# A decode step's cache loads: thirteen key tiles ahead of the projection, nine per group, and value tiles of all kinds interleaved

## What is computed

```python
def mix_sample(x, win_k, win_v, sb_k_pool, sb_v_pool, mem_k, mem_v, page_table, mw):
    ...
    qa, ka, va, qb, kb, vb, qm = project_heads(rms_norm(x, g_pre), w_in)
    ...
    o_a = combine_by_denominators([dilated_group_gather(qa, k_all, v_all, n_buf, w, d) for w, d in DIL_PATTERNS])
    k_past = sb_k_pool[page_table].reshape(B, n_past, N_HEADS_SB, HEAD_DIM)
    v_past = sb_v_pool[page_table].reshape(B, n_past, N_HEADS_SB, HEAD_DIM)
    ...
    o_b = sweep_query_blocks(lambda q, qp: stick_breaking_block(q, kb_all, vb_all, qp, sb_bias), qb, pos)
    o_m = memory_attention(qm, mem_k, mem_v)
    y = mixer_output(x, o_a, o_b, o_m, g_out_a, g_out_b, g_out_m, w_out, g_post)
```

## Time and profile before

| | us |
|---|---|
| median of three runs | 2264.4 (2260.56 to 2265.96) |
| profiled execution, its own time | 2271.0 |
| its span, first to last instruction | 2269.2 |
| TensorE busy | 2153.5 (95%) |
| VectorE busy | 1340.9 (59%) |
| ScalarE busy | 919.0 (40%) |
| DMA, mean | 202 GB/s |

### The profile page before, as it was taken

One profiled execution on the slowest core, in us unless ns is written; L12 is line 12 of the kernel. 1 busy time (PEld: TensorE's weight loads), 2 busy tenths in 40 slices (PEclk: granted clock), 3 DMA queues, 4 the chain that ended last, 5 costly groups with the idle time before them and its releaser, 6 DMA issues.

```text
span 2269.2 us, 41305 instructions
## 1 busy us (share of the span) xinstructions
PE 2153.5 (95%) x16769; PEld 2042.6 (90%) x16769; DVE 1340.9 (59%) x3210; ACT 919.0 (40%) x1171; POOL 429.5 (19%) x369
## 2 busy tenths in 40 slices
PE   7999999999999999999967879899999999999996
PEld 6999999999999999999842339799999999999996
DVE  6555545555555686777783426575545565555656
ACT  3544434444343455343312414454434344343443
POOL 5200000000000043677501100440000000000004
PEclk9999999999999999999989979899999999999999
DMA  7454555555555546999999975345555555555551
GB/s 262 168 186 171 182 176 178 186 173 180 186 177 177 185 167 244 332 339 349 317 273 314 278 205 176 130 171 183 186 174 180 186 178 176 185 182 174 184 184 41
DMA packets 221536, 459.24 MB, mean 202 GB/s; under 512 B 11466, under 2 KB 12363, under 8 KB 220571
## 3 DMA queue, kind: packets, MB, share of 16 engines
q1 hardware_dynamic: 219874, 452.32, 59.2%
q0 software_dynamic: 1472, 4.29, 0.5%
HBM read 447.95 MB, written 8.62 MB: 201 GB/s over the span
## 4 chain that ended last, share of the span: by engine, by line
PE 49%; DMA 4%; DVE 3%; SPq 2%; issue 1%; POOL 1%; ACT 0%; POOLq 0%; DVEq 0%; ACTq 0%
PE ps L503 15%; PE ps L505 15%; PE ps L504 15%; DMA v_cache<-win_v 1%; SPq L427 1%; PE ps L809 1%; DMA v_cache<-sb_v 1%; SPq L426 1%; PE ps L684 1%; POOL acc L1736 1%; DVE y L1288 1%; DVE k_cache L1453 1%; DMA v_cache<-mem_v 1%; DMA k_cache<-win_k 0%; PE ps L782 0%
## 5 line engine op out<-in xcount | busy, mean ns | idle before, releaser
L1242 DVE TENSOR_TENSOR wl<-raw,wh 128x1024 fp32r<-128x1024 f32 x592 | 732.9, 1243 | 703.7 <-ACT wh L889 702.8
L889 ACT ACTIVATE wh<-raw 128x1024 fp32r<-128x1024 f32 x656 | 691.6, 1059 | 1029.6 <-PE ps L505 1005.1
L503 PE MATMUL ps<-xh,wh 128*128 128x264 f32 (+1 forms) x3776 | 1081.3, 286 | 17.7 <-DVE xl L1254 9.4
L505 PE MATMUL ps<-xh,wl 128*128 128x264 f32 (+1 forms) x3776 | 1077.9, 285 | 0.0
L504 PE MATMUL ps<-xl,wh 128*128 128x264 f32 (+1 forms) x3776 | 1077.8, 285 | 0.0
L503 PEld LDWEIGHTS ps<-xh,wh 128*128 128x128 f32 x3776 | 715.2, 189 | 20.8 <-issue 9.0
L505 PEld LDWEIGHTS ps<-xh,wl 128*128 128x128 f32 x3776 | 715.4, 189 | 0.0
L504 PEld LDWEIGHTS ps<-xl,wh 128*128 128x128 f32 x3776 | 714.9, 189 | 0.2
L503 PE MATMUL ps<-hh,wh 128*128 128x264 f32 x1408 | 400.8, 285 | 0.0
L505 PE MATMUL ps<-hh,wl 128*128 128x264 f32 x1408 | 399.9, 284 | 0.0
L504 PE MATMUL ps<-hl,wh 128*128 128x264 f32 x1408 | 399.1, 283 | 0.0
(11 more groups left out here) (227 smaller groups left out, 1159.8 us busy)
## 6 DMA issues: line engine op xcount, KB each, us to landing
raw<-w_gu SPq DMA_DIRECT2D x176, 1024.0 KB, 4.9
raw<-w_down SPq DMA_DIRECT2D x88, 1024.0 KB, 5.0
raw<-w_in SPq DMA_DIRECT2D x40, 1024.0 KB, 7.5
v_cache<-sb_v SPq DMA_DIRECT2D x128, 256.0 KB
k_cache<-sb_k SPq DMA_DIRECT2D x84, 256.0 KB
raw<-w_out SPq DMA_DIRECT2D x16, 1024.0 KB, 5.4
head_space<-sb_k SPq DMA_DIRECT2D x44, 256.0 KB
raw<-w_mem_kv SPq DMA_DIRECT2D x8, 1024.0 KB, 5.4
```

Of the source, the lines that this page charges most:

```text
L503: pe.matmul(out, w_hi, rh(k0 + kk), start=first and kk == 0, stop=False)
L505: mm = pe.matmul(out, w_lo, rh(k0 + kk), start=False, stop=last and kk == 1)
L889: act.activation(wh[:, c % UNIT_SLOTS], raw_unit(c), ACT.Copy).then_inc(hi_made, 1)
L1242: dve.tensor_tensor(wl[:, c % UNIT_SLOTS], raw_unit(c), wh[:, c % UNIT_SLOTS].bitcast(F32), ALU.subtract).then_inc(lo_made, 1)
```

## The change

- `FIRST_KEYS` = 13 key tiles are loaded before the steady part. Seven of them (2 to 8, `key_place` "early") have buffers of their own that are used once: three where `mem_space` was, four in the space of the feed-forward part's intermediates. Four tiles (0 to 3) are issued behind chunks 4 to 7 of the memory weights, tiles 4 to 8 behind projection chunks 0 to 4, tiles 9 to 12 after the parking.
- In the steady part three tiles instead of two follow every fourth chunk: nine for a group. VectorE takes projections after the tiles in `TAKE_AT`.
- Spreads 2 to 17 stand inside groups, ahead of the unit that `SPREAD_AT` names (group, unit); 18 to 31 stay behind the last group.
- `value_tile` mixes the kinds: two page tiles of sequence b + 1, then one window or memory tile of sequence b, and so on. There are ten value slots, the last three (`late_values`) over `k_cache` (the first load into them waits for all keys), and three banks for sums instead of two.

```diff
-ADD_AT = (11, 13, 19, 21, 35, 37, 43, 45)
+ADD_AT = (15, 17, 24, 26, 43, 45, 52, 54)
+TAKE_AT = (11, 20, 29, 39, 48, 57, 66, 74)
+SPREAD_AT = {2: (3, 0), 3: (3, 7), 4: (4, 6), 5: (5, 5), 6: (6, 4), 7: (7, 3), 8: (8, 2), 9: (8, 4), 10: (8, 5),
+             11: (8, 6), 12: (8, 7), 13: (9, 0), 14: (9, 1), 15: (9, 3), 16: (9, 5), 17: (9, 6)}
...
-V_SLOTS = 7
+FIRST_KEYS = 13
+V_SLOTS = 10
...
+def key_user(t):
+
+    if t >= FIRST_KEYS + K_SLOTS:
+        return t - K_SLOTS
+    return t - FIRST_KEYS if t < FIRST_KEYS + 2 else t - FIRST_KEYS + 7
...
 def value_tile(t):
 
-    if t < SB_TILES:
-        return divmod(t, PAGES // 2)
-    b, k = divmod(t - SB_TILES, 4)
-    return b, PAGES // 2 + k
+    if t < PAGES // 2:
+        return 0, t
+    b, r = divmod(t - PAGES // 2, 12)
+    if b == DEC - 1:
+        return b, PAGES // 2 + r
+    return (b + 1, r // 3 * 2 + r % 3) if r % 3 < 2 else (b, PAGES // 2 + r // 3)
...
-            for n in range(8):
-                load_pair(CH_MEM + n, n, w_mem_kv[0], slice(0, 2))
...
+            for n in range(8):
+                load_pair(CH_MEM + n, n, w_mem_kv[0], slice(0, 2))
+                if n == 4:
+                    sp.wait_ge(const_loaded, 16 * 9)
+                    sp.wait_ge(xl_ready["mem"], KT)
+                if n >= 4:
+                    load_keys(n - 4)
+            sp.wait_ge(unit_used, unit_of(CH_MEM))
             for n in range(10):
                 load_in(n)
-            sp.wait_ge(const_loaded, 16 * 9)
-            sp.wait_ge(xl_ready["mem"], KT)
-            for t in range(2):
-                load_keys(t)
+                if n < 5:
+                    load_keys(n + 4)
...
-            for t in range(2, K_SLOTS):
+            for t in range(9, FIRST_KEYS):
                 load_keys(t)
-            t = K_SLOTS
+            t = FIRST_KEYS
             for n in range(12, 44):
                 load_in(n)
-                load_keys(t)
-                load_keys(t + 1)
-                t += 2
+                for _ in range(3 if n % 4 == 3 else 2):
+                    load_keys(t)
+                    t += 1
...
             for t in range(TILES):
+                if t == V_SLOTS - 3:
+                    sp.wait_ge(k_used, TILES)
                 if t >= V_SLOTS:
                     sp.wait_ge(v_weighed, t - V_SLOTS + 1)
...
-                pe.wait_ge(in_read, 8 if f < 8 else 20 if f < 16 else 40)
+                pe.wait_ge(in_read, 8 if f < 8 else 20 if f < 18 else 40)
...
-                if k in (0, PAGES // 2) and number >= 2:
-                    pe.wait_ge(sum_taken, number - 1)
+                if k in (0, PAGES // 2) and number >= 3:
+                    pe.wait_ge(sum_taken, number - 2)
...
-            for t in range(SB_TILES):
+            for t in range(TAKE_AT[7] + 1):
                 take_scores(t)
-                if t % 8 == 7:
-                    take_projection(2 + t // 8)
+                if t in TAKE_AT:
+                    take_projection(2 + TAKE_AT.index(t))
```

More of the change, by code:

```diff
@@ L192, in decoder_step @@
             mask_far = sb("mask_far", [P, 2, SEQ], F32, part)
+        with ExitStack() as part:
+            early_a = sb("early_a", [P, 2, 1024], F32, part)
+            sb("first_keys_kept", [P, 1120], F32, part)
+            early_b = sb("early_b", [P, 2, 1024], F32, part)
         kv = sb("kv", [P, 24, TOK])
@@ L196, in decoder_step @@
             mem_space = sb("mem_space", [P, KT, N_MEM], F32, part)
+        with ExitStack() as part:
+            early_v = sb("early_v", [P, 3, 1024], F32, part)
         with ExitStack() as part:
@@ L250, in decoder_step @@
         k_loaded = [sem(f"k_loaded{i}") for i in range(K_SLOTS)]
+        early_loaded = [sem(f"early_loaded{i}") for i in range(2)]
         v_loaded = [sem(f"v_loaded{i}") for i in range(V_SLOTS)]
@@ L512, in group @@
                 for c in range(8):
-                    if c == 5 and between is not None:
-                        between()
+                    if between is not None:
+                        between(c)
                     unit(v + c, c % UNIT_SLOTS, lambda k: xh[:, k, 0:width], lambda k: xl[:, k, 0:width],
@@ L579, in gate_up @@
                     group(v, TOK, 0, g_done[l], g_guard)
-                    group(v + 8, TOK, 4, u_done[l], u_guard, between=(lambda: turn_memory(s - 2)) if memory else None)
+                    group(v + 8, TOK, 4, u_done[l], u_guard, between=(lambda c: turn_memory(s - 2) if c == 5 else None) if memory else None)
                     if memory:
@@ L664, in free, with spread_inside @@
                     pe.wait_ge(in_read, max(8, 4 * g + j - 5))
-                group(g * 8 + u_in, TOK, [block_bank(g, j) for j in range(4)], in_done, free)
+                def spread_inside(c):
+                    for f, at in SPREAD_AT.items():
+                        if at == (g, c):
+                            spread(f)
+                group(g * 8 + u_in, TOK, [block_bank(g, j) for j in range(4)], in_done, free, spread_inside)
             def spread(f):
@@ L699, in _ @@
                 in_group(g)
-                spread(g)
             pe.wait_ge(roped, 8)
@@ L704, in _ @@
             for f in range(10, 32):
-                spread(f)
+                if f >= 18:
+                    spread(f)
                 r = f - 10
@@ L808, in weigh_values @@
                         by = zm[:, j].rearrange("p b h -> p (b h)")
-                    mm = pe.matmul(ps[5 + number % 2][32 * q:32 * q + 32, :], by, values, start=first, stop=last)
+                    mm = pe.matmul(ps[5 + number % 3][32 * q:32 * q + 32, :], by, values, start=first, stop=last)
                 mm.then_inc(v_weighed, 1)
@@ L1416, in take_projection @@
                 turned = g in TURNED_GROUPS
+                if g == TURNED_GROUPS[0]:
+                    dve.wait_ge(k_used, 9)
                 if turned and g > TURNED_GROUPS[0]:
@@ L1477, in _ @@
                               heads_first(kv[:, 0:H_WIN, SEQ:TOK]), ALU.mult).then_inc(new_prod, 1)
-            for t in range(SB_TILES, SB_TILES + DEC + 11):
+            for t in range(TAKE_AT[7] + 1, SB_TILES + DEC + 11):
                 take_scores(t)
@@ L1605, in take_sums @@
                     dve.wait_ge(sum_taken, number)
-                    kind, b = divmod(number, DEC)
-                    total, part = sums[:, kind], ps[5 + number % 2][:]
+                    kind, b = SUM_ORDER[number]
+                    total, part = sums[:, kind], ps[5 + number % 3][:]
                     if b == 0:
```

41 lines of the change are left out of this document (31 added, 10 removed).

## The result

The changed kernel took **2250.5 us** (median of 5 runs, 2246.2 to 2254.7), the kernel before beside it 2266.0 us (5 runs, 2260.6 to 2271.0): a ratio of 0.9935, 95% interval 0.9914 to 0.9956. The forecast was 2249 us in 2236 to 2268. The profiled execution took 2254.7 us (span 2252.9), against 2271.0 (span 2269.2).

A forecast was written before the change was run, and what follows sets the result against it. It took TensorE to bound the projection (DMA level with it), then VectorE's key scoring, then value loads. Terms -1.2 and -14 summed to -15 us, giving 2249 us at the median, range 2236 to 2268.

The forecast's parts named there:

- Early keys: Seven more key tiles loaded beside memory weights and first projection chunks, where the DMA share was about 0.5: cost nothing.
- Nine tiles a group: Projection groups: VectorE takes 75 key tiles instead of 64, 18.8 us out of 57.7 us of waiting; priced at 0.
- Spreads: Projection: nine more spreads on PE, 8.0 us, plus 2.1 us waiting at spread 13; it ends 10.1 us later.
- Tail of the keys: After the last projection: 18.8 us less scoring, 7.5 us new wait; with the later start, first value page -1.2 us.
- Values: Value stretch: mixing page tiles with window and memory tiles, with ten slots, keeps the queue full; taken as -14 us.
- The list of what would show it: Signs of right steps, among them last take 10 us later, first value page 1160 to 1164, VectorE never idle for k tiles.
- DMA alone, -9: Bound on the value stretch: pages at 327 GB/s, windows and memory at 240, 5 us landing: 169 us against 178.
- Rival: the queue bounds the projection: Projection groups need 367 GB/s against 353 at full share, so chunks come late: +8, result -7 us, 2257 us; chance 0.13.
- Rival: mixing brings the values to TensorE's pace, -26: Value stretch: mixing speeds window rows to the pages' 327 GB/s, values -25, result -26 us, 2238 us; chance 0.15.
- Rival: window rows drag the pages with them: Value stretch: pages queue behind slow window rows, all at one rate; at 255 GB/s +15 us, 2279 us; chance 0.14.
- the break-even of 277: Value stretch: the common rate in GB/s for all 48.2 MB below which the change loses.
- Rival: nothing moves: Spreads and tail cancel, and the mixed value stream runs at about 280 GB/s: 2262 us; chance 0.13.

The follow-up runs named there:

- values_alone: The kernel before with only the value half of the change (mixed order, ten slots, three banks), keys as they were: 2249.8 us, ratio 0.9941.
- keys_alone: The changed kernel with value tiles in the old order and seven value slots, three banks kept, so only the key half stands: 2264.0 us, ratio 1.0004.
- old_order_half_weighing: The changed kernel with the old value order and half the page tiles weighed over 32 columns in place of 512: 2257.0 us, ratio 0.9970.
- old_order_half_lookups: The changed kernel with the old value order and each value tile's second page a fixed one, not looked up: 2243.5 us, ratio 0.9905.
- tail_and_later_spread: The changed kernel with spreads 18 to 23 issued earlier around the turned rows, and spreads 13 and 14 one group member later: 2247.7 us, ratio 0.9925.
- lookups_in_pairs: tail_and_later_spread with both page numbers of a tile read before its two transfers are issued, for keys and values: 2247.7 us, ratio 0.9925.
- old_value_order: The changed kernel with value tiles by kind again (64 page tiles, then 32 of windows and memory), ten slots and three banks kept: 2260.0 us, ratio 0.9988.

## Why the prediction was right, step by step

- **Early keys, 0.** Held. 233 and 260 GB/s at 800 to 860 us with TensorE at 30.00 and 26.97 us, as before.
- **Nine tiles a group, 0.** Held. No wait of TensorE for wl from 912 to 1110 us. But the cover got thin where it was put: ScalarE, which splits the weight chunks, now waits for them to land, and didn't before. The waits of that stretch:

```profile
ACT wh L956 <- DMA raw<-w_in: 63.7, 20, 4.7
POOL wl L1867 <- ACT wh L956: 53.7, 43, 8.0
DVE by_sin L1492 <- PE ps L567: 16.0, 4, 5.9
DVE kv L1495 <- PE ps L567: 12.1, 8, 6.7
DVE k_cache L1522 <- PE ps L751: 10.0, 4, 5.0
DVE qT L1495 <- PE ps L567: 5.8, 4, 4.9
PE ps L751 <- DVE kv L1495: 3.8, 1, 3.8
PEld ps L751 <- issue: 2.5, 1, 2.5
PE ps L751 <- DVE zm L1522: 2.3, 1, 2.3
```

- **Spreads, +8.0 and 2.1 at spread 13.** Held: the last take ends 10.0 us later, forecast 10.1, and the last row above is spread 13's wait, 2.3. That it agrees to a tenth is luck: the whole stretch began 0.75 us sooner (takes 0 and 1 at 908.85 us, before 909.60), so the projection itself got 10.7 us longer. Moving that spread by one member gave 2.0 us back. The list of what would show it had no idle time of VectorE for key tiles; for the *tiles* that held, but VectorE waited 10.0 us for spreads up to 1110 us and another 8.7 for spread 17 (until 1113.60 us), which the text hadn't priced. It was air: VectorE's waits for TensorE's blocks fell from 57.7 to 33.9 us (16.0 + 12.1 + 5.8).
- **Tail of the keys, -1.2.** The wait of 7.5 us was there with 7.1, at the spread named. The first page came 3.1 us sooner, of which 0.75 was the earlier start. That leaves 2.4: the projection cost 0.6 more than forecast, and the tail behind it shrank by 13.1 us and not by 11.3. Against the trace of *values_alone*, which has the old key half too, it is 1.4. The medians of *keys_alone*, 1.0004 (0.9988 to 1.0020), don't tell -1.2 from 0.
- **Values, -14.** The size was near: -11.6 in the profile (166.5 against 178.1), and -11.5 between the medians of *values_alone* and the before (-13 by their ratio, 0.9941). The range that it came from had the wrong ends, and this is the step that failed in kind; that a number taken between them came out near is in good part luck. The end "DMA alone, -9" took 327 GB/s as the pages' rate at a full share; with half the lookups (and half the pages in fixed places) they ran at 386. So 327 wasn't what the queue could do. The text named two causes of the pages' pace in one breath, "SyncE's 0.8 us a page and PE's slots". They are far from equal. In the kernel before, SyncE waited for a slot for 6.1 of the 110.7 us of page issues:

```profile
SPq L426 <- PE ps L809: 6.1, 8, 4.2
```

With ten slots this is gone (1.1 us, 105.9 us for the pages), and *old_order_half_weighing* doesn't shorten them further; *old_order_half_lookups* takes a part of the first cause away and they fall to 89.4. The extra slots, counted with the mixing, are worth nothing once it is there. And the reason given for going beyond -9, that window rows come faster when mixed, isn't shown by any run: the *new* order gained nothing over the old one once issues were cheap. Why window and memory tiles move slower than pages at all, no run shows.

- **Rival: the queue bounds the projection.** False. It took 353 GB/s for the full queue, where windows had shown up to 371; the rate went to 387 at share 1.05 from 1058 to 1083 us. The Trainium skill's 358 GB/s for one core ("DMA: Bandwidth & Descriptors", Specifications), by which a group would have taken 24.9 us, is passed by that row too.
- **Rival: mixing brings the values to TensorE's pace, -26.** Not so. TensorE's waits for landing value tiles sank from 36.7 us (22.8 + 9.5 + 3.8 + 0.6) to 27.0, of which this is the largest row of after, from 1160 to 1331 us:

```profile
PE ps L876 <- DMA v_cache<-sb_v: 14.6, 15, 2.4
```

- **Rival: window rows drag the pages with them.** Not in the sense that decides (the mixed stretch ran at 293 to 322 GB/s, over the break-even of 277), but its mechanism fits the end of the study: pages alone 386 GB/s at a full queue, mixed 326 and 307. Weighing 33.55 MB at 386 and 14.7 MB at the 246 GB/s that window rows had alone before gives 87 + 60 = 147 us, an average of 329 GB/s. Mixed, from 1200 to 1280 us, it was 326 and 307, about 4% less. It is an estimate from few windows: in *values_alone* the same windows have 330 and 315, 2% less, so it may be no loss at all.
- **Rival: nothing moves.** Half of it came true: spreads and tail do about cancel. The mixed stream ran over its 280 GB/s, and the gain is there.

## What to carry to other kernels

When a stretch shows a DMA share just below full and every consumer with some waits, count the *issues* before the bytes: the number of issues times the issuing engine's time for one is a third bound, beside the queue and the engine that uses the data, and a gather with a table lookup per transfer is where it bites. Interleaving cheap issues that carry slow bytes with costly issues that carry fast ones hides such a bound (here 0.5% of the kernel); it doesn't remove it, and halving the lookups showed that more lay there than the order could give. And compare traces by distances from a mark near the edit: here they are good to tenths of a us up to the first value page, while the value stretch behind it differs by 8 us between executions of one value part, and a saving of 2 or 3 us ahead of it can't be followed through.

The best version with everything computed was *tail_and_later_spread* at 2247.7 us, 3 us under the changed kernel, which the intervals can't tell apart. A version in which another engine looks up or issues a part of the pages wasn't tried.

## What the hardware showed that wasn't expected

- One page issue with its lookup costs SyncE 0.81 to 0.83 us when nothing holds it: 0.27 the register load (median 266 ns), 0.33 the issue, and the rest between them. Without a lookup of its own an issue follows the one before in 0.52 us (*lookups_in_pairs*), so a lookup adds 0.3. The Trainium skill ("Runtime: NRT & Kernel Launch", Instruction fetch mechanics) has about 200 ns for a register load of this kind; the rows of *old_value_order* have 262 at the least, and two in a row don't overlap (*lookups_in_pairs*).
- The core's queue moved 386 and 387 GB/s over 24 and 25 us beside a full TensorE, at share 1.05, and 386 over 40 us from pages alone (*old_order_half_lookups*, half of them in fixed places).
- Window and memory tiles alone ran at 246 GB/s at share 1.01 to 1.04 in the kernel before (1274 to 1325 us):

```profile
1274.00:1300.00 26.00, 21.92 (x89) 8.45 (x88) 12.19 (x23) 8.82 (x22) 4.26 (x6) 0.87 1.01 246
1300.00:1325.00 25.00, 18.69 (x72) 5.00 (x72) 5.56 (x12) 2.96 (x10) 2.50 (x4) 0.93 1.04 246
```
